# A hybrid decoder block in one core: who requests the down products' weights, and where the activations land

## The chip, the cores and the metric

The kernel runs on one NeuronCore of a Trainium2 chip. The metric is the device time of one execution in microseconds. All times are read from executions on the chip: three runs for the time, and one profiled execution for the trace.

The five engines run side by side and meet only at semaphores. TensorE (PE) multiplies, ScalarE (ACT) and VectorE (DVE) work on rows of tiles, GpSimd (POOL) and SyncE (SP) here mostly request transfers. A transfer is requested by an engine in its own program order: an engine that waits for a semaphore requests nothing that stands behind the wait.

## The reference

The reference is one decoder layer on 2048 tokens of width 1024, in float32: attention, a gated chunk mixer and a state-space layer, an output projection, then a gated feed-forward part with a causal convolution, a gated embedding and a last normalisation. The change touches only the feed-forward part:

```python
def conv_ffn(x, w_up, conv_w, conv_b, w_down):
    h = x @ w_up                      # 2048x1024 @ 1024x5632
    h = lax.conv_general_dilated(h, conv_w[:, None, :], ...) + conv_b
    val, gate = jnp.split(h, 2, axis=-1)
    return (jax.nn.gelu(gate) * val) @ w_down   # 2048x2816 @ 2816x1024
...
    h = h + conv_ffn(rms_norm(h, norm_ffn_g[i]), ffn_w_up[i], ffn_conv_w[i],
                     ffn_conv_b[i], ffn_w_down[i])
```

## The kernel before

Every float32 operand of a product is split in two float32r tiles, hi (a rounded copy, by ACT) and lo (the rest, by DVE), and each product is three matmuls: hi by hi, hi by lo, lo by hi.

`feed_forward` works in two halves of 1024 tokens. Each half has an up part and a down part.

The **up part** goes over 22 features (128 columns of value and 128 of gate each). A feature is seven products of twelve matmuls (kinds 1 to 7, a Strassen-like scheme over two token groups and two halves of the depth), in an order that `FIRST` gives for the first feature and `products` for the rest. Kinds 3, 4, 5, 6 and 7 take their activation operand from tiles of their own, `x3` to `x7` (a hi and a lo half each; the lo half holds the exact value until it is overwritten). Sums of weights are made in `sums`. The results go through the convolution in `strips` and are stored to DRAM (`ffn_act`) from `late` by POOL, two stores a feature.

The **down part** is four passes (two token groups by two halves of the 1024 output columns). A pass goes over the 22 features; each is twelve matmuls on four banks. The weights come in units of four features, 1 MB each, six units a pass (the last has two features, 0.5 MB). They land in `w`, two buffers that units take in turn; a unit is split by `split_unit` (one ACT and one DVE instruction) into one of two regions of `ring`, which is free once the last feature of the unit before last is multiplied. The activations of a feature, 256 KB, are loaded from `ffn_act` (`load_a`) and split by `split_a` into one of four slots (`a_hi`, `a_lo`; tiles `a_early` and `a_late`). The buffer that an activation lands in (`a_exact`) is the same memory as the slot's lo half: the split overwrites it in place, and PE reads it. So the load of activation a+4 waits until PE has finished feature a (`wait_feature_done`).

What sets the order of the work around the change is written out by hand, one program per engine:

- SP requests in one sequence the weights (`load_w_after`, which waits until the unit that held the buffer is split, `w_lo_ready`), the activations (`load_a`), the residual rows of each pass (`load_resid`, 1 MB, in the unit j = 2), in half 0 the input rows of the next half (`load_rows`, 2 MB each, at two places), and in half 1 ahead of pass 1 the eight 512 KB pieces of the weights of the last stage (`w_gate_loads`, 4 MB).
- ACT and DVE split activations `AHEAD` = 2 features ahead of the one whose turn it is, with the unit split (`split_unit` of the next unit) ahead of them at the start of each unit. At the end of the up part (`j == N - 1`) they split the first four (`RING`) activations before the last feature's convolution is done.
- PE waits for the unit's and the activation's lo half (`w_lo_ready`, `a_lo_ready`).
- POOL stores the activations of the half, then one 1 MB result per pass.

Half 0's down part also prepares half 1: the rows are squared, scaled, turned by PE (`turn`, eight times eight transposes in passes 1 and 3) and split; the last three operands, kinds 6, 7 and 4, in `split_sums`.

Of the kernel before, what the change touches and what calls it, by code (L numbers as in the profile page):

```python
# [22 lines left out]
P = 128  # L23
# [1637 lines left out]
def feed_forward(nc, h1, gain, w_up, conv_w, conv_b, w_down, h2, act_rows, w_gate_loads, shared, ident):  # L1661
# [45 lines left out]
    LO_NEEDED = {1: 2 * KH, 2: 2 * KH, 5: 4 * KH, 3: 4 * KH, 6: 4 * KH + 1, 7: 4 * KH + 2, 4: 4 * KH + 3}  # L1707
# [4 lines left out]
    with Stage(nc, "ffn") as st:  # L1712
        halves_of = shared.rearrange("p (o s k t) -> p o s k t", o=2, s=2, k=KH)
        own, exact = {}, {}
        for kind in (3, 4, 5, 6, 7):
            own[kind] = st.sb(f"x{kind}", [P, 2, KH, BANK], F32R)
            exact[kind] = st.over(f"exact{kind}", [P, KH, BANK], F32, nc.sbuf_base - KH * BANK * 4)
        x_hi = {1: halves_of[:, 0, 0], 2: halves_of[:, 1, 0], **{kind: t[:, 0] for kind, t in own.items()}}
# [21 lines left out]
        a_exact = [sums[:, 1], sums[:, 3], plain[:, BANK:2 * BANK], plain[:, 3 * BANK:4 * BANK]]  # L1740
# [7 lines left out]
        w_loaded = st.sems("w_loaded", 2)  # L1748
# [7 lines left out]
        a_loaded = st.sems("a_loaded", RING)  # L1756
# [17 lines left out]

        def loads_through(W):
            return sum((2 if v % UNITS < F else 1) for v in range(W % 2, W + 1, 2)) * DMA

        def wait_raw(engine, W):
            engine.wait_ge(w_loaded[W % 2], loads_through(W))
# [26 lines left out]
        def last_of_half(h):  # L1806
            return (h + 1) * PASSES * F
# [22 lines left out]

        @block.sync
        def _(sp):
# [4 lines left out]
            def load_w(W):  # L1837
                h, u = divmod(W, UNITS)
                if u < F:
                    for n in range(2):  # L1840
                        col = (n * F + u) * P
                        sp.dma_start(w_raw[W % 2][:, n], up_cols[:, :, col:col + P]).then_inc(w_loaded[W % 2], DMA)
                else:
                    p, j = divmod(u - F, PER_PASS)
                    fs, cols = unit_features[j], slice(p % NH * BANK, (p % NH + 1) * BANK)
                    flat = w_raw[W % 2].rearrange("p n k c -> p (n k c)")[:, 0:len(fs) * BANK]
                    sp.dma_start(flat.rearrange("p (f c) -> p f c", c=BANK), down_rows[:, fs[0]:fs[-1] + 1, cols]).then_inc(w_loaded[W % 2], DMA)

            def load_w_after(W):
# [893 lines left out]
```

## Time and profile before

| | us |
|---|---|
| median of 3 runs | 2889.83 (2889.22 to 2890.85) |
| the profiled execution | 2886.86 |
| its span, first to last instruction | 2885.3 |
| TensorE busy in the span | 2607.5 (90%) |
| VectorE, ScalarE, GpSimd busy | 1712.4, 1368.2, 509.6 |
| down part of half 0 | 1659.0 to 1923.2 |
| down part of half 1 | 2345.0 to 2605.0 |
| last stage | from 2605.0 |

The profiled execution is 3.0 us below the median of the runs, with 1.6 us around its span. Times within the span are counted from its first instruction. A row of the timeline gives the start, the duration, the engine, the line, what it writes and reads, and in brackets the idle time before it with what ended it. Matmuls are pipelined: their durations overlap, and the distance between two starts tells the rate.

### The profile page before, as it was taken

To read this page: it belongs to the slowest core of one execution; us is meant where nothing else is said; L and a number is where in the kernel's file an instruction comes from. 1 tells how busy PE (TensorE), PEld (TensorE's weight loads), DVE (VectorE), ACT (ScalarE), POOL (GpSimd) and SP (SyncE) were. 2 spreads that over 40 slices of the span, in tenths; PEclk is the share of its full clock that TensorE was granted. 3 is DMA by queue.
4 is the path that set the end of the run, shared out by engine and by line. 5 is a ranking of instruction groups with operands and counts; after the bars stand their busy time and mean duration, and the time that the engine had idled before them with its cause. 6 is when DMAs were issued, how large, how long until landed. Compare 5 with 4: busy or idle time off the path is not lost. (4 is left out here: it accounts for less than half of the span.)

```text
span 2885.3 us, 38789 instructions
## 1 busy us (share of the span) xinstructions
PE 2607.5 (90%) x13883; PEld 2239.3 (78%) x13883; DVE 1712.4 (59%) x3358; ACT 1368.2 (47%) x2460; POOL 509.6 (18%) x309
## 2 busy tenths in 40 slices
PE   6999997999845799489999999999999998997998
PEld 5989986999834588478888777778888876775876
DVE  1110272777596776488888755578888864444333
ACT  3343332666423666455555444455555542334444
POOL 3454454666300121000000000000000000000000
PEclk9999998999977799789999999999999999998999
DMA  4665456888333253312222366642222246662221
GB/s 163 195 213 172 152 170 157 188 185 185 70 100 126 87 182 129 104 59 88 88 81 75 116 208 232 224 146 88 88 81 75 87 152 245 223 205 99 79 76 46
DMA packets 313909, 392.09 MB, mean 136 GB/s; under 512 B 22161, under 2 KB 222161, under 8 KB 310650
## 3 DMA queue, kind: packets, MB, share of 16 engines
q1 hardware_dynamic: 299850, 341.60, 39.2%
q0 software_dynamic: 13888, 48.25, 4.3%
q8 instruction: 103, 1.69, 0.2%
q14 instruction: 68, 0.56, 0.1%
HBM read 298.59 MB, written 95.33 MB: 137 GB/s over the span
## 5 line engine op out<-in xcount | busy, mean ns | idle before, releaser
L2355 PE MATMUL ffn_bank<-ffn_x,ffn_ring 128*128 128x512 f32 x880 | 346.0, 393 | 19.1 <-DVE ffn_ring L2149 13.6
L2356 PE MATMUL ffn_bank<-ffn_x,ffn_ring 128*128 128x512 f32 x880 | 345.4, 393 | 0.0
L2357 PE MATMUL ffn_bank<-ffn_x,ffn_ring 128*128 128x512 f32 x880 | 345.4, 392 | 0.0
L504 ACT ACTIVATE att_exps<-att_scores,att_part 128x256 f32<-128x256 f32 (+1 forms) x384 | 153.1, 454 | 124.4 <-DVE att_part L475 121.7
L2355 PEld LDWEIGHTS ffn_bank<-ffn_x,ffn_ring 128*128 128x128 f32 x880 | 166.8, 190 | 55.8 <-DVE ffn_ring L2149 9.1
L475 DVE CUSTOM_DVE_ANT_0 att_scores<-att_bank,att_bias 128x256 f32<-128x256 f32 (+1 forms) x384 | 122.5, 363 | 141.3 <-PE att_bank L422 66.1
L2422 POOL DMA_DIRECT2D ffn_act<-ffn_late x88 | 47.6, 541 | 858.7 <-DVE ffn_late L2201 858.7
L2188 DVE SCALAR_TENSOR_TENSOR ffn_strips<-ffn_strips,ffn_taps 128x512 f32<-128x512 f32 x176 | 132.0, 750 | 111.9 <-ACT ffn_strips L1999 111.9
L938 POOL TENSOR_TENSOR in_w_lo<-in_w,in_w_hi 128x2048 fp32r<-128x2048 f32 x36 | 166.0, 4612 | 183.3 <-ACT in_w_hi L821 183.3
L2357 PEld LDWEIGHTS ffn_bank<-ffn_x,ffn_ring 128*128 128x128 f32 x880 | 166.8, 190 | 34.9
L2356 PEld LDWEIGHTS ffn_bank<-ffn_x,ffn_ring 128*128 128x128 f32 x880 | 166.9, 190 | 34.5
L908 PE MATMUL in_bank<-in_w_hi,in_hi 128*128 128x256 f32 x640 | 184.6, 288 | 0.7 <-issue 0.7
L909 PE MATMUL in_bank<-in_w_lo,in_hi 128*128 128x256 f32 x640 | 183.2, 286 | 0.0
L910 PE MATMUL in_bank<-in_w_hi,in_lo 128*128 128x256 f32 x640 | 183.2, 286 | 0.0
L1985 ACT COPY ffn_strips<-ffn_bank 128x512 f32<-128x512 f32 x176 | 103.3, 587 | 141.8 <-PE ffn_bank L2357 141.8
L449 PE MATMUL att_bank<-att_v,att_expsT 128*128 128x66 f32 x1200 | 153.1, 269 | 1.9 <-DVE att_expsT L486 1.3
L1956 ACT CAST ffn_ring<-ffn_sums 128x512 fp32r<-128x512 f32 x176 | 108.0, 614 | 94.5 <-PE ffn_bank L2357 83.8
L2387 PE MATMUL ffn_bank<-ffn_ring,ffn_a_late 128*128 128x512 f32 x352 | 139.8, 397 | 13.9 <-DVE ffn_a_late L2163 13.8
L2387 PE MATMUL ffn_bank<-ffn_ring,ffn_a_early 128*128 128x512 f32 x352 | 139.8, 397 | 11.2 <-DVE ffn_a_early L2163 11.1
L2157 DVE TENSOR_TENSOR ffn_ring<-ffn_w,ffn_ring 128x2048 fp32r<-128x2048 f32 (+1 forms) x48 | 101.5, 2114 | 81.0 <-ACT ffn_ring L1965 80.9
L449 PEld LDWEIGHTS att_bank<-att_v,att_expsT 128*128 128x128 f32 x1200 | 146.6, 192 | 3.7 <-DVE att_expsT L486 2.0
L2355 PE MATMUL ffn_bank<-tail_shared,ffn_ring 128*128 128x512 f32 x352 | 138.0, 392 | 1.0 <-DVE ffn_ring L2149 1.0
(337 smaller groups left out, 7004.0 us busy)
## 6 DMA issues: line engine op xcount, KB each, us to landing
ffn_w<-in_ffn_w_up SPq DMA_DIRECT2D x88, 512.0 KB, 4.7
ffn_w<-in_ffn_w_down SPq DMA_DIRECT2D x40, 1024.0 KB, 7.1
in_w<-in_w_in SPq DMA_DIRECT2D x36, 1024.0 KB, 6.2
ffn_act<-ffn_late POOLq DMA_DIRECT2D x88, 256.0 KB, 2.7
ffn_sums<-ffn_act SPq DMA_DIRECT2D x88, 256.0 KB, 4.5
ffn_strips<-ffn_act SPq DMA_DIRECT2D x88, 256.0 KB, 4.5
mixed_part<-branch_results SPq DMA_DIRECT2D x16, 792.0 KB, 5.3
z_rows<-in_result SPq DMA_DIRECT2D x80, 128.0 KB, 2.5
```

Of the source, the lines that this page charges most:

```text
L449: mm = pe.matmul(out, expsT[:, n % 2, piece * P:(piece + 1) * P], vals[:, b, blk, h * ROW:(h + 1) * ROW], start=(at == 0), stop=(at == len ...
L475: nc.vector.tensor_tensor_reduce(scores[:, n % RING, m * width:(m + 1) * width], score_bank[n % 3][:, m * width:(m + 1) * width], bias[pai ...
L504: nc.scalar.activation(exps[:, n % RING, m * width:(m + 1) * width], scores[:, n % RING, m * width:(m + 1) * width], ACT.Exp, bias=part[:, ...
L908: pe.matmul(out[:, 0:WIDE], x_hi[:, k, part], w_hi[w][:, k, :], start=(k == 0), stop=False)
L909: pe.matmul(out[:, 0:WIDE], x_hi[:, k, part], w_lo[w][:, k, :], start=False, stop=False)
L910: mm = pe.matmul(out[:, 0:WIDE], x_lo[:, k, part], w_hi[w][:, k, :], start=False, stop=(k == KC - 1))
L938: nc.gpsimd.tensor_tensor(w_lo[B % 2][:, :, :], w_raw[B % 2][:, :, :], w_hi[B % 2][:, :, :].bitcast(F32), ALU.subtract).then_inc(w_lo_read ...
L2188: nc.vector.scalar_tensor_tensor(conv[:, n, tg], raw[f % 2][:, n, 1 + tg * BANK:1 + (tg + 1) * BANK], tap[1], conv[:, n, tg], ALU.mult, AL ...
L2355: pe.matmul(out[:, :], hi[:, k], x_hi[kind][:, k], start=(k == 0 and fresh), stop=False, skip_group_check=not fresh)
L2356: pe.matmul(out[:, :], hi[:, k], x_lo[kind][:, k], start=False, stop=False, skip_group_check=not fresh)
L2357: mm = pe.matmul(out[:, :], lo[:, k], x_hi[kind][:, k], start=False, stop=(k == KH - 1), skip_group_check=not fresh)
L2387: pe.matmul(out, a_hi[r][:, toks], ring[:, first + i], start=(f == 0), stop=False)
```

## The change

The activations get landing buffers of their own, `a_raw`: four buffers of 256 KB in the memory of the hi half of `x6`, which no product reads from the last kind 6 product of the up part on. The split reads `a_raw` and writes the slot. A load now waits only until the activation four before it is split (`a_lo_ready`), and the wait for PE moves from the load to the split (ACT, in `split_a`). `AHEAD` becomes 3, and three instead of four activations are split at the end of the up part; the fourth comes in the down part, behind `split_unit` of unit 1.

The weights of the down units from the third on, and the first two up weights of half 1, are requested by POOL (`load_w_after(pool, ...)`), behind its last activation store of the half; the pass results are stored behind the second such request of the next pass. The loads have two semaphores per queue. SP keeps the activations, the residual rows and the input rows. The eight pieces of the last stage's weights are no longer requested in a row but one per unit (j other than 2) from the start of pass 1 of half 1.

Since `x6` is taken until the last activation of half 0 is split, its `split_sums` comes last of the three in half 1 (`LAST_SUMS`), two features later than before (`FINISH_AT`), and the first feature of half 1 runs its kinds in the order 1, 5, 2, 3, 6, 7 instead of 1, 5, 6, 3, 2, 7.

```diff
-    AHEAD = 2
+    AHEAD = 3
     RING = 4
+    RAW = 4
...
-    TURN_AT, FINISH_AT = (2, 6, 10, 14), (15, 17, 18, 19)
-    FIRST = ((1, 2, 5, 3, 6, 7), (1, 5, 6, 3, 2, 7))
+    TURN_AT, FINISH_AT = (2, 6, 10, 14), (15, 17, 18, 20)
+    FIRST = ((1, 2, 5, 3, 6, 7), (1, 5, 2, 3, 6, 7))
+    LAST_SUMS = ((6, 7, 4), (7, 4, 6))
...
+            if kind == 6:
+                a_raw = st.over("a_raw", [P, RAW, BANK], F32, nc.sbuf_base - 2 * KH * BANK * 4)
...
-        a_exact = [sums[:, 1], sums[:, 3], plain[:, BANK:2 * BANK], plain[:, 3 * BANK:4 * BANK]]
...
-        w_loaded = st.sems("w_loaded", 2)
+        w_loaded = [st.sems("w_loaded_sp", 2), st.sems("w_loaded_pool", 2)]
...
+        def by_pool(W):
+            return int(W >= 2 and (W - 2) % UNITS >= F)
...
+        def load_w_after(queue, W):
+            h, u = divmod(W, UNITS)
+            if W + 2 < HALVES * UNITS:
+                queue.wait_ge(w_lo_ready, operand_count(h, at[h][u, 4]) if u < F else unit_count(h, u - F))
+                load_w(queue, W + 2)
...
             def load_a(a):
                 h, p, f = feature(a)
                 o = (h * F + f) * TG + p // NH
-                r = a % RING
-                if a >= h * PASSES * F + RING:
-                    wait_feature_done(sp, *divmod(a - RING, F))
-                elif r < 2:
-                    sp.wait_ge(w_lo_ready, operand_count(h, at[h][F - 1, 7]))
+                if a >= h * PASSES * F + RAW:
+                    sp.wait_ge(a_lo_ready, a - RAW + 1)
                 else:
-                    sp.wait_ge(conv_ready, (h * F + F - 1) * 4)
+                    sp.wait_ge(product_done, h * N + at[h][F - 1, 6] + 1)
                 sp.wait_ge(act_stored[o % RING], (o // RING + 1) * DMA)
                 col = h * PART + p // NH * BANK
-                sp.dma_start(a_exact[r], act_rows[f][:, col:col + BANK]).then_inc(a_loaded[r], DMA)
+                sp.dma_start(a_raw[:, a % RAW], act_rows[f][:, col:col + BANK]).then_inc(a_loaded[a % RAW], DMA)
...
-                    if h + 1 == HALVES and p == 1:
-                        sp.wait_ge(product_done, HALVES * N)
-                        for part, src, loaded in w_gate_loads:
-                            sp.dma_start(part, src).then_inc(loaded, DMA)
                     for j, fs in enumerate(unit_features):
-                        load_w_after(h * UNITS + F + p * PER_PASS + j)
                         for f in fs:
-                            a = (h * PASSES + p) * F + f + RING
+                            a = (h * PASSES + p) * F + f + RAW
...
+                        if h + 1 == HALVES and p in (1, 2) and j != 2 and p * PER_PASS + j < 2 * PER_PASS + 4:
+                            n = (p - 1) * (PER_PASS - 1) + j - (j > 2)
+                            part, src, loaded = w_gate_loads[n]
+                            if n == 0:
+                                sp.wait_ge(product_done, HALVES * N)
+                            sp.dma_start(part, src).then_inc(loaded, DMA)
...
             def split_a(a):
-                r = a % RING
-                act.wait_ge(a_loaded[r], (a // RING + 1) * DMA)
-                nc.scalar.copy(a_hi[r], a_exact[r]).then_inc(a_hi_ready, 1)
+                h, p, f = feature(a)
+                act.wait_ge(a_loaded[a % RAW], (a // RAW + 1) * DMA)
+                if a >= h * PASSES * F + RING:
+                    wait_feature_done(act, *divmod(a - RING, F))
+                elif a % RING < 2:
+                    act.wait_ge(w_lo_ready, operand_count(h, at[h][F - 1, 7]))
+                else:
+                    act.wait_ge(conv_ready, (h * F + F - 1) * 4)
+                nc.scalar.copy(a_hi[a % RING], a_raw[:, a % RAW]).then_inc(a_hi_ready, 1)
...
                     if j == N - 1:
-                        for a in range(first, first + RING):
+                        for a in range(first, first + AHEAD):
                             split_a(a)
...
                 for p in range(PASSES):
-                    store(h * PASSES + p)
+                    for j in range(PER_PASS):
+                        load_w_after(pool, h * UNITS + F + p * PER_PASS + j)
+                        if p and j == 1:
+                            store(h * PASSES + p - 1)
+                store(h * PASSES + PASSES - 1)
```

Three places of the instruction order follow, of before and of the change apart.

SP in half 1, from the request of a unit in pass 0 to pass 1. `tail_w_gate` is the last stage's weights, `ffn_late` the residual rows; `ffn_sums` and `ffn_strips` are the old landing buffers of the activations. Before:

```order
L1847 DMA ffn_w<-in_ffn_w_down 128x4x512
L1867 DMA ffn_sums<-ffn_act 128x512 x2
L1899 DMA tail_w_gate<-in_ple_w_gate 128x1024 x8
L1847 DMA ffn_w<-in_ffn_w_down 128x4x512
L1867 DMA ffn_strips<-ffn_act 128x512 x2
```

And in the change, all of SP's requests from unit j = 2 of pass 0 to unit j = 3 of pass 1:

```order
L1880 DMA ffn_late<-after_mixers 128x4x512
L1870 DMA ffn_a_raw<-ffn_act 128x512 x14
L1914 DMA tail_w_gate<-in_ple_w_gate 128x1024
L1870 DMA ffn_a_raw<-ffn_act 128x512 x4
L1914 DMA tail_w_gate<-in_ple_w_gate 128x1024
L1870 DMA ffn_a_raw<-ffn_act 128x512 x4
L1880 DMA ffn_late<-after_mixers 128x4x512
L1870 DMA ffn_a_raw<-ffn_act 128x512 x4
L1914 DMA tail_w_gate<-in_ple_w_gate 128x1024
```

The requests of weights are gone from SP, and the eight pieces stand one by one between groups of activations.

POOL in the whole feed-forward part. Before it holds the load of the gain and the stores alone:

```order
L2431 DMA ffn_gain<-in_norm_ffn_g 128x8x1
L2422 DMA ffn_act<-ffn_late 128x512 x44
L2428 DMA after_ffn<-ffn_late 128x4x512 x4
L2422 DMA ffn_act<-ffn_late 128x512 x44
L2428 DMA after_ffn<-ffn_late 128x4x512 x4
```

In the change, from the up part of half 1 on, passes 0 and 1:

```order
L2434 DMA ffn_act<-ffn_late 128x512 x44
L1847 DMA ffn_w<-in_ffn_w_down 128x4x512 x3
L1847 DMA ffn_w<-in_ffn_w_down 128x2x512
L1847 DMA ffn_w<-in_ffn_w_down 128x4x512 x4
L2440 DMA after_ffn<-ffn_late 128x4x512
L1847 DMA ffn_w<-in_ffn_w_down 128x4x512
L1847 DMA ffn_w<-in_ffn_w_down 128x2x512
```

The first request of a weight unit stands behind the 44th store of the half.

ACT at the end of the up part and the start of the down part. `ffn_a_early` and `ffn_a_late` are the slots (two each), `ffn_ring<-ffn_w` with 2048 columns is a unit's split, the rows with `ffn_taps` and `ffn_strips` are the last feature's convolution and gelu. Before:

```order
L1965 CAST ffn_ring<-ffn_w 128x2048
L1971 CAST ffn_a_early<-ffn_sums 128x512 x2
L1971 CAST ffn_a_late<-ffn_strips 128x512 x2
L1999 ACTIVATE ffn_strips<-ffn_strips,ffn_taps 128x512 x2
L1985 COPY ffn_strips<-ffn_bank 128x512
L1999 ACTIVATE ffn_strips<-ffn_bank,ffn_taps 128x512
L1999 ACTIVATE ffn_strips<-ffn_strips,ffn_taps 128x512
L2004 ACTIVATE ffn_strips<-ffn_strips 128x512 x2
L1965 CAST ffn_ring<-ffn_w 128x2048
L1971 CAST ffn_a_early<-ffn_sums 128x512 x2
```

In the change:

```order
L1971 CAST ffn_ring<-ffn_w 128x2048
L1983 CAST ffn_a_early<-ffn_a_raw 128x512 x2
L1983 CAST ffn_a_late<-ffn_a_raw 128x512
L2011 ACTIVATE ffn_strips<-ffn_strips,ffn_taps 128x512 x2
L1997 COPY ffn_strips<-ffn_bank 128x512
L2011 ACTIVATE ffn_strips<-ffn_bank,ffn_taps 128x512
L2011 ACTIVATE ffn_strips<-ffn_strips,ffn_taps 128x512
L2016 ACTIVATE ffn_strips<-ffn_strips 128x512 x2
L1971 CAST ffn_ring<-ffn_w 128x2048
L1983 CAST ffn_a_late<-ffn_a_raw 128x512
L1983 CAST ffn_a_early<-ffn_a_raw 128x512 x2
```

The fourth activation has moved from ahead of the last convolution to behind the split of unit 1. DVE has the same order.

## Rows read from the trace of the kernel before

**Rows 1.** Windows of the down parts: PE, PEld, DVE, ACT, POOL, clock, DMA, GB/s.

```profile
1659.00:1923.20 264.20, 253.16 (x1121) 206.12 (x1119) 151.90 (x177) 126.33 (x168) 3.35 (x5) 0.99 0.64 213
...
2345.00:2605.00 260.00, 244.79 (x1057) 199.22 (x1055) 118.69 (x132) 93.04 (x112) 3.35 (x5) 0.97 0.62 210
```

**Rows 2.** The timeline of PE around the down parts.

```profile
1900.35 1.04 PE L2324 MATMUL ffn_bank<-whole_ident,ffn_strips 128*128 128x128 f32 x8
...
1923.29 0.51 PE L2355 MATMUL ffn_bank<-tail_shared,ffn_ring 128*128 128x512 f32 x1 [1.03 <-DVE ffn_ring L2149]
...
2344.99 0.39 PE L2387 MATMUL ffn_bank<-ffn_ring,ffn_a_early 128*128 128x512 f32 x1
...
2350.43 0.39 PE L2387 MATMUL ffn_bank<-ffn_ring,ffn_a_late 128*128 128x512 f32 x1
...
2428.08 0.77 PE L2387 MATMUL ffn_bank<-ffn_ring,ffn_a_late 128*128 128x512 f32 x1 [10.01 <-DVE ffn_a_late L2163]
```

**Rows 3.** Waits of PE: us in total, times, longest; half 0's down part.

```profile
PE ffn_bank L2387 <- DVE ffn_a_early L2163: 7.6, 5, 4.0
PE ffn_bank L2387 <- DVE ffn_a_late L2163: 2.2, 2, 1.9
```

**Rows 4.** The same view of waits, half 1's down part.

```profile
PE ffn_bank L2387 <- DVE ffn_a_late L2163: 11.6, 3, 10.0
PE ffn_bank L2387 <- DVE ffn_a_early L2163: 3.5, 5, 1.4
```

**Rows 5.** Windows around the two longest waits of PE.

```profile
2412.00:2430.00 18.00, 7.70 (x29) 6.01 (x30) 4.89 (x9) 3.40 (x4) 0.76 (x1) 0.73 1.01 396
2428.00:2434.00 6.00, 5.92 (x14) 4.72 (x15) 4.06 (x4) 2.68 (x3) 0.00 (x0) 0.52 0.32 123
1685.00:1700.00 15.00, 14.98 (x59) 12.27 (x60) 5.60 (x7) 7.07 (x9) 0.00 (x0) 0.89 0.37 125
```

**Rows 6.** Waits of ACT in half 1's down part.

```profile
ACT ffn_a_late L1971 <- DMA ffn_strips<-ffn_act: 78.6, 26, 15.4
```

**Rows 7.** The timeline of ACT and DVE at the start of half 0's down part.

```profile
1664.16 1.90 ACT L1965 CAST ffn_ring<-ffn_w 128x2048 fp32r<-128x2048 f32 x1
...
1666.09 2.29 DVE L2157 TENSOR_TENSOR ffn_ring<-ffn_w,ffn_ring 128x2048 fp32r<-128x2048 f32 x1 [1.04 <-ACT ffn_ring L1965]
1668.30 1.35 DVE L2163 TENSOR_TENSOR ffn_a_early<-ffn_sums,ffn_a_early 128x512 fp32r<-128x512 f32 x2
```

**Rows 8.** The timeline of SP's requests ahead of the two longest waits.

```profile
1670.50 1.93 SPq L1835 DMA_DIRECT2D ffn_strips<-after_mixers  x4
...
1673.72 2.17 SPq L1867 DMA_DIRECT2D ffn_sums<-ffn_act  x2
...
2405.99 4.37 SPq L1899 DMA_DIRECT2D tail_w_gate<-in_ple_w_gate  x8
```

**Rows 9.** DMA issues of the page: KB each, median us to landing.

```profile
ffn_w<-in_ffn_w_down SPq DMA_DIRECT2D x40, 1024.0 KB, 7.1
ffn_act<-ffn_late POOLq DMA_DIRECT2D x88, 256.0 KB, 2.7
after_ffn<-ffn_late POOLq DMA_DIRECT2D x8, 1024.0 KB, 6.2
```

**Rows 10.** All instances of two lines: min, median, max duration in ns.

```profile
L2428 POOL DMA_DIRECT2D after_ffn<-ffn_late x8: 752/756/762, 1734.7 to 2608.3; - x8
L2088 DVE TENSOR_SCALAR ffn_strips<-ffn_strips,ffn_rstd x14: 747/748/754, 1187.3 to 1849.8; 128x1024 f32<-128x1024 f32 x14
```

**Rows 11.** POOL's last store of half 0's up part.

```profile
1665.35 0.54 POOL L2422 DMA_DIRECT2D ffn_act<-ffn_late  x1 [0.32 <-DVE ffn_late L2201]
```

**Rows 12.** DVE at the start of half 1's down part.

```profile
2354.91 1.29 DVE L2163 TENSOR_TENSOR ffn_a_early<-ffn_sums,ffn_a_early 128x512 fp32r<-128x512 f32 x2
```

**Rows 13.** DVE just before the up part of half 1.

```profile
1917.69 2.29 DVE L2120 TENSOR_TENSOR ffn_x<-ffn_exact,ffn_x 128x2048 fp32r<-128x2048 f32 x1
```

**Rows 14.** PE in the first feature of half 0.

```profile
1249.43 0.47 PE L2355 MATMUL ffn_bank<-ffn_x,ffn_ring 128*128 128x512 f32 x1 [0.77 <-ACT ffn_strips L1985]
```

More of the change, by code:

```diff
@@ L1706, in feed_forward @@
     LO_HALF, SUM_HALF = 4 * KH + 3, 3 * KH + 1
-    LO_NEEDED = {1: 2 * KH, 2: 2 * KH, 5: 4 * KH, 3: 4 * KH, 6: 4 * KH + 1, 7: 4 * KH + 2, 4: 4 * KH + 3}
+    LO_NEEDED = [{1: 2 * KH, 2: 2 * KH, 5: 4 * KH, 3: 4 * KH, **{kind: 4 * KH + n + 1 for n, kind in enumerate(last)}} for last in LAST_SUMS]
     up_cols = w_up.rearrange("(k p) n -> p k n", p=P)
@@ L1773, in unit_count @@
             return h * (N + DOWN_UNITS) + N + u + 1
+        def by_pool(W):
+            return int(W >= 2 and (W - 2) % UNITS >= F)
         def loads_through(W):
-            return sum((2 if v % UNITS < F else 1) for v in range(W % 2, W + 1, 2)) * DMA
+            return sum((2 if v % UNITS < F else 1) for v in range(W % 2, W + 1, 2) if by_pool(v) == by_pool(W)) * DMA
         def wait_raw(engine, W):
-            engine.wait_ge(w_loaded[W % 2], loads_through(W))
+            engine.wait_ge(w_loaded[by_pool(W)][W % 2], loads_through(W))
         def wait_feature_done(engine, n, f):
@@ L1835, in load_rows @@
                     sp.dma_start(rows_of(h, grp, t), row_tiles[(h * TG + grp) * TILES + t]).then_inc(rows_loaded[grp][t], DMA)
[L1837 to L1849, printed above, removed]
-                h, u = divmod(W, UNITS)
-                if W + 2 < HALVES * UNITS:
-                    sp.wait_ge(w_lo_ready, operand_count(h, at[h][u, 4]) if u < F else unit_count(h, u - F))
-                    load_w(W + 2)
             def load_a(a):
@@ L1942, in split_sums @@
             def split_sums(h, n):
-                act.wait_ge(x_summed, h * SUM_HALF + 3 * KH + (1 if n == 2 else 0))
-                kind = (6, 7, 4)[n]
+                kind = LAST_SUMS[h][n]
+                act.wait_ge(x_summed, h * SUM_HALF + 3 * KH + (1 if kind == 4 else 0))
+                if h and kind == 6:
+                    act.wait_ge(a_lo_ready, last_of_half(h - 1))
                 nc.scalar.copy(x_hi[kind], exact[kind][:, :, :]).then_inc(hi_written, 1)
@@ L2032, in _ @@
                     if j == N - 1:
-                        for a in range(first, first + RING):
+                        for a in range(first, first + AHEAD):
                             split_a(a)
@@ L2117, in split_sums @@
             def split_sums(h, n):
-                kind = (6, 7, 4)[n]
+                kind = LAST_SUMS[h][n]
                 dve.wait_ge(hi_written, h * LO_HALF + 4 * KH + n + 1)
@@ L2248, in _ @@
                     if j == N - 1:
-                        for a in range(first, first + RING):
+                        for a in range(first, first + AHEAD):
                             split_a(a)
```

28 lines of the change are left out of this document (20 added, 8 removed).

## The prediction

> **What bounds the kernel now.** I read the windows first. The two down parts take 264.2 and 260.0 us with PE at a granted clock of 0.99 and 0.97 and the DMA engines busy 64% and 62% of the time [rows 1]. In the timeline, 24 down matmuls start from 2344.99 to 2350.43, so one takes 0.2267 us [rows 2]; 4 passes of 22 features of 12 matmuls are 1056, or 239.4 us. Half 0 has eight turns on top, 1.04 us each [rows 2], 8.3 us. What is left is loss: 264.2 - 239.4 - 8.3 = 16.5 us, and 260.0 - 239.4 = 20.6 us, together 37.1 us.
>
> Then the waits of PE. It waits for the activations' split only, never for a down unit: 7.6 + 2.2 = 9.8 us in half 0 [rows 3], 11.6 + 3.5 = 15.1 us in half 1 [rows 4], and 1.03 us for the first weight operand of half 1 [rows 2]: 25.9 us. Behind the two long waits the granted clock falls to the lower level (1.2 instead of 2.4 GHz): 0.52 over 6 us is 2.9 us lost, 0.89 over 15 us is 1.7 us [rows 5]. The last 6.6 us are small gaps and restarts.
>
> Then who is late. ACT in half 1 waits for activations to land, 78.6 us in 26 waits for one kind of slot [rows 6]: DVE and ACT are not the bound, the transfers are. The reason is the loop: activation a+4 is requested when PE has finished a, and has three features, 3 x 2.72 = 8.2 us, to land and be split; with ACT's and DVE's share 1.3 us (DVE's two splits in 1.35 us [rows 7], so 0.7 each) some 6.8 us for landing. The longest waits stand behind bursts: the eight pieces of 4 MB requested at 2405.99 to 2410.36, with the DMA engines at 1.01 and 396 GB/s, end in PE's 10.01 us; 2 MB of rows at 1670.50, one row of the queue ahead of the activations at 1673.72, end in the 4.0 us of half 0 [rows 2, 3, 5, 8].
>
> **The change, part by part.** *Landing buffers and three ahead.* The request of a+4 now follows the split of a, which ACT may do when PE has finished a-4. So it goes out some 7 features less a split ahead of its use, 19 - 1.4 = 17.7 us, instead of 8.2. The split itself can start three features (8.2 us) ahead of its use. At a unit's start ACT splits the unit (1.90), DVE too (2.29), then the activation (0.7) [rows 7]: 4.9 us, inside 8.2; before it was inside 5.4, which is where the waits under 2 us come from. I cost these waits at nothing left, except for remainders below.
>
> *Weights by POOL.* A unit is requested when the one in its buffer is split, some 4.9 us after the start of the unit before; ACT wants it at the second unit start from there, 2 x 10.9 - 4.9 = 16.9 us later. A load by POOL doesn't occur in this stretch; the nearest rows are its stores of the same 1 MB and pieces, 0.756 us to issue and 6.2 us to land, against 7.1 for SP's load of a unit [rows 9, 10]. I take 6 to 7 us; under 16.9 it costs nothing. At the start of a down part POOL comes to its first request behind the last store, at 1665.35 + 0.54 = 1665.9 [rows 11]. Landed by 1673, split by 1678; PE wants it at feature 8, 1659.0 + 21.8 = 1680.8. Hidden, by 3 us. But 1 MB now moves into the time of the 2 MB of rows: with unit 3 and the activations 4.5 MB from 1665.9, 11.4 us at 396 GB/s [rows 5], until 1677.3. Activation 8 lands there, and PE wants it at 1680.8 plus the delay below. I cost it at nothing, at most 4.
>
> *Eight pieces apart.* A unit of 10.9 us then carries 1 MB of weights, 1 MB of activations and 0.5 MB: 240 GB/s of the 396 seen. The 10.01 us and the 2.9 us of clock go.
>
> *Three instead of four splits at the start.* This one costs. The fourth activation stands behind unit 1's split on DVE, where the fifth stood: ready at 1668.30 + 0.68 = 1669.0 [rows 7]. PE wants it at 1659.0 + 8.2 = 1667.2: a wait of 1.8 us. In half 1: 2354.91 + 0.7 = 2355.6 against 2345.0 + 8.2 = 2353.2, 2.4, less 0.6 for the split that no longer stands ahead of DVE's unbroken chain: 1.8 [rows 12]. Together 3.7 with the semaphores.
>
> *Half 1's start.* DVE's third 2.29 us split stood at 1917.69, just ahead of the sums of the first weights [rows 13]; it moves behind the first operands, so the 1.03 us wait goes. Kinds 6 and 7 now follow each other on one bank, as in half 0, where PE waited 0.77 us for ACT's copy of the bank between them [rows 14]: +0.9 with the restart.
>
> *Sum.* 37.1 lost now; left are 3.7 + 0.9, and I keep 2.5 of the small gaps and of clock behind the two new waits (bounds: 0, and the 6.6 + 4.6 that stand there now). 37.1 - 7.1 = 30.0 gained. The profiled execution of 2886.9 becomes 2856.9; the median of the runs stands 3.0 above it: 2859.8, say 2860. Own range 2852 to 2871.
>
> On the second queue, the trace shows the engines full at 396 GB/s when SP alone requests [rows 5]. The Trainium skill (DMA: Bandwidth & Descriptors, "Issuing engines are not separate DMA queues") says that transfers of all issuing engines run on the same 16 DMA engines and that another issuer saves only issue time. By that rule the queue split gives no bandwidth; the sum would stand, since it rests on earlier requests, or fall to rival 1 if they give nothing.
>
> **Rivals.** 1: *the transfers stay as late as they are.* Waits come from full engines, and asking earlier only queues more: the small waits stay, only the burst of 4 MB is spread. That saves 10.0 + 2.9 and costs 3.7 + 0.9: 8.3 gained, 2881 or 2882; with half the small waits gone 2875. For it: 64% mean load with bursts, and a burst at half 0's start that is now 1 MB fuller. Against it: between the bursts 213 GB/s is half of what the engines did, and the loop's 8.2 us explains the small waits without any shortage.
>
> 2: *POOL's loads land late* (the slower side). If a unit takes L from request to landing, two units need L + 4.9 us per buffer, and PE needs on average 19.9 us for two (a pass is 59.8 us for six units). From L = 15 on each us costs 22 us over the 22 pairs. At L = 17 that is 44 - 30: 2904; at 20, 2970; at 16.4 the gain is eaten. For it: no load of this shape by POOL is in the trace, and DVE works all through. Against it: POOL's 88 stores took a median of 2.7 us with DVE at its busiest, and the 1 MB stores 6.2 [rows 9]; L would have to be more than double. The Trainium skill (SBUF — State Buffer, "SBUF: two separate sides") speaks for it: a DMA requested by GpSimd has its descriptors written by GpSimd, which a VectorE operation in a two-port mode locks out until it ends. What could do so here are the row scalings, four in a row of 0.75 us twice in half 0 [rows 10]: 3.0 us late on a unit that has 10 to spare, so by the rule the sum stands; it would need the same from the 2.29 us splits to bring this rival in, and for these the page says there is no two-port mode.
>
> 3: *the gain is given back at the starts.* The first units and activation 8 come late in both halves by up to 4 us each, the clock falls behind each wait (1.7 each), and some small waits stay: 2884 to 2890. For it: margins of 3 us at the start. Against it: in half 1 no rows are loaded there.
>
> **How the numbers follow.** Forecast 0.70; rival 1 0.14 (2873 to 2882); rival 3 0.07; rival 2 0.09. A difference under 0.2% (5.8 us) can't be told from none. Faster: forecast, rival 1 and a fifth part of the others, with a little off for what I haven't seen, 0.84; same 0.07; slower 0.09. The range that leaves out 2 in 10 is 2850 to 2882: below it would lie only a sum in which no loss at all remains and the up parts gain too.
>
> **What would show it.** Right: in PE's waits the down parts hold one wait of about 1.8 us each at feature 3 and next to nothing else; the parts take about 250 and 243 us; the 10 us wait is gone and the granted clock is 0.99 or more in both; POOL's loads of a unit land in 6 to 8 us; a wait of 0.8 us between kinds 6 and 7 in half 1. Wrong: PE waits for `ffn_ring` of a unit in the down parts (rival 2), or ACT still waits some 50 us for landings with PE's small waits in place (rival 1), or a wait of several us at features 7 to 9 of half 0 (rival 3).

## The result and the profile after

The changed kernel takes 2856.12 us in the median of five runs (2854.08 to 2860.05), against 2889.83 before: 0.9886 of the time, with a 95% interval of 0.9871 to 0.9900. Run again later on another occasion, it took 2856.95 against 2889.53 (0.9891, 0.9875 to 0.9908). The profiled execution took 2856.12 us, 30.7 less than the profiled one of before; the forecast for it was 30.0 less. Among all executions behind this document a single one, of the kernel e6 below, took 6817 us; it is left out of the numbers.

The windows of the down parts in the changed kernel; behind the length stand the busy times of PE, weight loads, DVE, ACT and POOL, then the granted clock, the DMA share and GB/s. They answer to [rows 1, 5]; the third is the start of half 0's down part.

```profile
1658.00:1911.10 253.10, 249.02 (x1121) 205.71 (x1120) 150.49 (x178) 126.96 (x167) 23.32 (x31) 0.99 0.67 224
2333.70:2575.10 241.40, 239.66 (x1057) 197.96 (x1055) 117.98 (x132) 93.77 (x113) 19.76 (x27) 1.00 0.67 228
1665.00:1684.00 19.00, 15.24 (x66) 11.96 (x65) 8.11 (x8) 5.15 (x8) 2.13 (x3) 1.00 0.96 356
```

The parts take 253.1 and 241.4 us where they took 264.2 and 260.0: 29.7 of the 30.7 us. Over what the matmuls and turns need (247.7 and 239.4), 5.4 and 2.0 us are left of 37.1. Outside the down parts, the first down product starts 1.0 us earlier (1658.0 against 1659.0), the up part of half 1 is 0.9 us longer (422.6 against 421.7), and the last stage, from the end of the down part to the end of the span, is 0.9 us shorter (279.3 against 280.2).

All waits of PE from the last product of the first up part to the end of the second down part, in its timeline:

```profile
1653.59 0.47 PE L2367 MATMUL ffn_bank<-ffn_x,ffn_ring 128*128 128x512 f32 x1 [2.36 <-DVE ffn_strips L2185]
...
1668.01 0.50 PE L2399 MATMUL ffn_bank<-ffn_ring,ffn_a_late 128*128 128x512 f32 x1 [1.66 <-DVE ffn_a_late L2175]
...
1684.33 0.47 PE L2399 MATMUL ffn_bank<-ffn_ring,ffn_a_early 128*128 128x512 f32 x1 [2.42 <-DVE ffn_a_early L2175]
...
1925.63 0.47 PE L2367 MATMUL ffn_bank<-ffn_x,ffn_ring 128*128 128x512 f32 x1 [0.77 <-ACT ffn_strips L1997]
...
2330.82 0.47 PE L2367 MATMUL ffn_bank<-ffn_x,ffn_ring 128*128 128x512 f32 x1 [2.36 <-DVE ffn_strips L2185]
...
2343.72 0.50 PE L2399 MATMUL ffn_bank<-ffn_ring,ffn_a_late 128*128 128x512 f32 x1 [1.74 <-DVE ffn_a_late L2175]
```

Of sixteen waits in and between the down parts [rows 2 to 4] four are left: the fourth activation at each start (1668.01, 2343.72), activation 8 (1684.33), and kind 7 behind kind 6 (1925.63). The two of 2.36 us close the up parts; they were there before.

Who is waited for on ACT, half 1's down part (total us, times, longest), against [rows 6]:

```profile
ACT ffn_ring L1971 <- PE ffn_bank L2401: 43.6, 21, 2.1
ACT ffn_a_late L1983 <- PE ffn_bank L2401: 32.5, 21, 2.1
ACT ffn_a_early L1983 <- PE ffn_bank L2401: 26.3, 18, 2.1
ACT ffn_a_early L1983 <- DMA ffn_a_raw<-ffn_act: 16.6, 8, 3.3
ACT ffn_a_late L1983 <- DMA ffn_a_raw<-ffn_act: 12.4, 8, 3.4
```

Beside the 78.6 us of [rows 6], ACT had this wait for the other kind of slot before:

```profile
ACT ffn_a_early L1971 <- DMA ffn_sums<-ffn_act: 52.5, 24, 4.4
```

This is the view that tells what bounds the part: ACT waited 131.1 us for activations to land and now waits 29.0 us for them, but 102.4 us for PE.

The DMA issues (KB each, median us to landing), against [rows 9]:

```profile
ffn_a_raw<-ffn_act SPq DMA_DIRECT2D x176, 256.0 KB, 6.3
...
ffn_w<-in_ffn_w_down POOLq DMA_DIRECT2D x36, 1024.0 KB, 9.3
```

Both kinds of loads take longer from request to landing than before (an activation took 4.5 us, a unit 7.1), and it costs nothing where they are requested early enough.

### The profile page after: what moved, and what is told of

It is laid out like the page before. It is cut to its first block and busy times, and to the rows that moved or that the text cites. A ratio compares the mean times of both kernels' runs of the same rounds, so it can differ in the third digit from the quotient of the medians.

```text
span 2854.5 us, 38966 instructions
## 1 busy us (share of the span) xinstructions
PE 2597.1 (91%) x13883; PEld 2235.7 (78%) x13883; DVE 1710.4 (60%) x3358; ACT 1369.3 (48%) x2460; POOL 545.8 (19%) x357
## 5 line engine op out<-in xcount | busy, mean ns | idle before, releaser
L2399 PE MATMUL ffn_bank<-ffn_ring,ffn_a_early 128*128 128x512 f32 x352 | 138.5, 393 | 2.4 <-DVE ffn_a_early L2175 2.4
L2401 PE MATMUL ffn_bank<-ffn_ring,ffn_a_early 128*128 128x512 f32 x352 | 137.7, 391 | 0.0
## 6 DMA issues: line engine op xcount, KB each, us to landing
in_w<-in_w_in SPq DMA_DIRECT2D x36, 1024.0 KB, 6.2
ffn_w<-in_ffn_w_down POOLq DMA_DIRECT2D x36, 1024.0 KB, 9.3
```

Source lines behind the costliest of these rows:

```text
L2399: pe.matmul(out, a_hi[r][:, toks], ring[:, first + i], start=(f == 0), stop=False)
L2401: mm = pe.matmul(out, a_lo[r][:, toks], ring[:, first + i], start=False, stop=(f == F - 1))
```

## The experiments

Each was timed in alternation with the kernel before (medians 2891.1 for the first four, 2886.7 for the next four, 2889.5 for the last three). Runs of one kernel in one group differ by up to 9 us (2885.88 to 2895.05 for before in the first group). A part of this lies ahead of all that the edits touch: the first up product started between 1210.5 and 1215.9 us in the profiled executions. So an edit worth 2 or 3 us is read from the length of the down parts in one profiled execution each. They repeat more closely: the change gave 253.1 and 241.4 us once, 253.4 and 241.4 again, and before and e2, whose programs are the same in half 0, gave 264.3 and 265.5 there.

| kernel | median us | ratio to before (95%) | down part 0 | down part 1 |
|---|---|---|---|---|
| before | 2889.83 | | 264.3 | 260.0 |
| change | 2856.12 | 0.9886 (0.9871 to 0.9900) | 253.1 | 241.4 |
| e1 weights by SP | 2860.93 | 0.9894 (0.9879 to 0.9909) | 251.1 | 241.4 |
| e2 before, pieces apart | 2880.57 | 0.9958 (0.9944 to 0.9972) | 265.5 | 251.4 |
| e3 pieces in a row | 2858.28 | 0.9886 (0.9871 to 0.9901) | 253.6 | 243.9 |
| e4 four at the start | 2857.00 | 0.9878 (0.9863 to 0.9893) | 254.5 | 239.4 |
| e5 rows two and two | 2853.90 | 0.9888 (0.9872 to 0.9904) | 248.8 | 241.4 |
| e6 three edits | 2852.52 | 0.9882 (0.9863 to 0.9901) | 249.6 | 239.4 |
| e7 two ahead | 2861.62 | 0.9916 (0.9902 to 0.9930) | 253.5 | 246.9 |
| e8 before, three ahead | 2898.36 | 1.0039 (1.0025 to 1.0053) | 279.9 | 254.0 |
| change again | 2856.95 | 0.9891 (0.9875 to 0.9908) | 253.4 | 241.4 |
| e9 e6 with e1 | 2850.85 | 0.9870 (0.9853 to 0.9886) | 248.4 | 239.6 |
| e10 e9, unit behind add | 2849.08 | 0.9865 (0.9848 to 0.9881) | 250.7 | 241.6 |

The parts are measured from the first down matmul to the next part's first matmul (half 0), or to the end of the last one.

**e1: is the second queue worth anything?**

```diff
         def by_pool(W):
-            return int(W >= 2 and (W - 2) % UNITS >= F)
+            return 0
...
                     for j, fs in enumerate(unit_features):
+                        load_w_after(sp, h * UNITS + F + p * PER_PASS + j)
                         for f in fs:
...
                     for j in range(PER_PASS):
-                        load_w_after(pool, h * UNITS + F + p * PER_PASS + j)
```

> The change with the down units' weights back in SP's sequence, one request at the start of each unit as before; landing buffers, three ahead and the pieces apart stay. My theory (the gain comes from requesting an activation seven features ahead instead of three, and from the pieces apart; the second queue adds nothing by itself): SP reaches the request of a unit at about the time POOL does, some 4.9 us into the unit before, so the time stays within 3 us of the change, 2853 to 2859, with no waits of PE beyond the start waits; the wait of 2.4 us at feature 8 of half 0 gets shorter, since unit 2 is then requested before the rows. Rival (the separate queue is what does it): activations behind 1 MB units in one queue come late again, PE has its waits under 2 us back, 2866 or more.

Down part 1 is the same to the tenth, down part 0 is 2.0 us shorter. The median is 1.9 us over the upper end of what I expected; the profiled execution was already 4.1 us behind the change's at the first up product (1215.9 against 1211.8), where the two programs are the same, and this part is no effect of the queue. PE's waits in down part 0 (total us, times, longest):

```profile
PE ffn_bank L2400 <- DVE ffn_a_late L2176: 1.7, 1, 1.7
PE ffn_bank L2337 <- DVE ffn_late L2221: 0.8, 1, 0.8
PE ffn_bank L2337 <- issue: 0.6, 1, 0.6
PE ffn_bank L2400 <- DVE ffn_a_early L2176: 0.5, 1, 0.5
```

The wait for activation 8 fell from 2.42 to 0.5 us, and no small waits for activations came back; two waits of the turns (L2337), 0.8 and 0.6 us, are new. And its DMA issues:

```profile
ffn_a_raw<-ffn_act SPq DMA_DIRECT2D x176, 256.0 KB, 5.9
ffn_w<-in_ffn_w_down SPq DMA_DIRECT2D x40, 1024.0 KB, 6.9
```

With one queue a unit lands in 6.9 us, with POOL's in 9.3, and activations are not late behind units. The move of the weights to POOL's queue, by which the change is named, is not what gained the time; in the down parts the second queue brought no speed. What it may be worth lies in the last stage, about a microsecond: that stage took 279.0 to 279.3 us in the seven profiled kernels in which POOL requests the weights and 279.9 to 280.4 in the six in which SP does. Why was not looked into.

**e2: what are the pieces apart worth by themselves?** The kernel before, with the eight pieces requested as in the change:

```diff
-                    if h + 1 == HALVES and p == 1:
-                        sp.wait_ge(product_done, HALVES * N)
-                        for part, src, loaded in w_gate_loads:
-                            sp.dma_start(part, src).then_inc(loaded, DMA)
...
+                        if h + 1 == HALVES and p in (1, 2) and j != 2 and p * PER_PASS + j < 2 * PER_PASS + 4:
+                            ...
+                            sp.dma_start(part, src).then_inc(loaded, DMA)
```

> The kernel before, with only the eight 512 KB pieces requested one per unit from pass 1 of half 1 instead of in a row. My theory: the 10.0 us wait, its restart and the 2.9 us of low clock behind it go, the small waits stay and one or two grow: 12 to 14 us gained, 2876 to 2878. Rival (the buffers would have absorbed the burst anyway, or the pieces only move the wait): less than 6 us gained, or waits of 2 us at each of the eight pieces, 2884 or more. If nearly all of the gain came from here: 2862 or less.

The median fell by 10.6 us, under the 12 to 14 expected, and down part 1 by 8.6. The 10.01 us wait is gone, but 12.0 us of loss are left in the part. Its timeline of PE holds:

```profile
2431.60 0.47 PE L2389 MATMUL ffn_bank<-ffn_ring,ffn_a_late 128*128 128x512 f32 x1 [1.20 <-DVE ffn_a_late L2165]
...
2478.17 0.80 PE L2389 MATMUL ffn_bank<-ffn_ring,ffn_a_late 128*128 128x512 f32 x1 [2.63 <-DVE ffn_a_late L2165]
```

The first stands at a down feature where before had no wait, the second at one where before waited 1.15 us. Behind the second the granted clock fell:

```profile
2478.20:2488.20 10.00, 10.00 (x32) 7.99 (x32) 4.25 (x7) 2.57 (x3) 0.76 (x1) 0.69 0.57 195
```

That is 3.1 us more. It explains most of why the part gained 8.6 us and not the 10.0 + 2.9 of the long wait. That the pieces made these two activations late is likely but not shown: in half 0, where the two programs are the same, one wait went from 0.88 to 3.79 us between the two executions.

**e3: does the lead absorb the burst?** The change, with the eight requests in a row ahead of pass 1 of half 1 as before (the edit of e2 reversed).

> The change with the eight pieces requested in a row again, ahead of pass 1 of half 1. My theory: an activation is requested 17.7 us ahead, the burst of 4 MB takes about 11 us at 396 GB/s, with a unit and the activations in it 14 us; so PE waits 0 to 4 us in place of 10.0: 2856 to 2861. Rival (the burst costs what it cost before, whatever the lead): the wait of 10 us and its low clock are back, 2868 to 2870.

```profile
2411.79 0.47 PE L2397 MATMUL ffn_bank<-ffn_ring,ffn_a_late 128*128 128x512 f32 x1 [2.02 <-DVE ffn_a_late L2173]
```

It does: where the burst cost a wait of 10.01 us and 2.9 us of clock, it costs a wait of 2.02 us, and down part 1 is 2.5 us longer than the change's. The median can't tell it from the change (0.9886 of before for both). So the pieces apart are worth 8.6 us without the lead and 2.5 with it; the two edits overlap.

**e7: what does the third feature ahead do?** The change with `AHEAD = 2`.

> The change with activations split two features ahead instead of three (two at the end of the up part); landing buffers, POOL's requests and the pieces apart stay. My theory (the landing buffers carry most: a request goes out six features ahead instead of three, and the split needs 4.9 us of 5.4 behind a unit's split): PE gets waits under 1 us at some of the 44 unit starts, and the start wait is larger, since the third activation stands behind unit 1's split too: 4.4 us in each half, 2.7 more than now. Down parts 256 to 258 and 244 to 247: 2862 to 2869. Rival (three ahead is what does it, the buffers little): waits at most unit starts, 2876 or more.

Its timeline of PE in the down parts holds three waits, two of which are the starts:

```profile
1667.38 0.80 PE L2399 MATMUL ffn_bank<-ffn_ring,ffn_a_late 128*128 128x512 f32 x1 [4.38 <-DVE ffn_a_late L2175]
...
1899.82 0.50 PE L2399 MATMUL ffn_bank<-ffn_ring,ffn_a_early 128*128 128x512 f32 x1 [0.35 <-DVE ffn_a_early L2175]
...
2343.42 0.80 PE L2399 MATMUL ffn_bank<-ffn_ring,ffn_a_late 128*128 128x512 f32 x1 [4.40 <-DVE ffn_a_late L2175]
```

The start waits are the 4.4 us expected, and of the small waits one of 0.35 us is left. The ratio to before is 0.9916, where the change has 0.9886 and 0.9891. Down part 1 is 5.5 us longer than the change's: 2.7 us are the longer start wait, and the rest is the clock in the ten microseconds behind it, which in the change stays at 1.00:

```profile
2343.40:2353.40 10.00, 9.98 (x31) 7.98 (x32) 1.77 (x3) 1.32 (x1) 0.42 (x1) 0.69 0.88 290
```

From the fifth feature on each takes 2.72 us, as in the change. Down part 0 and the median (2861.62) came out a little under what I expected. So the buffers, with the requests as in the change, remove the small waits; the third feature ahead is worth the start wait and the clock behind it, and nothing in the steady part. In half 0 even that is hidden: what the start wait costs, the wait for activation 8, which is gone here, gives back (253.5 against 253.1 us).

**e8: three ahead without the buffers.** The kernel before with `AHEAD = 3`, in-place landing kept.

> The kernel before with the splits three features ahead instead of two, four at the start as before; activations still land in the slot's lo half, so their request waits for PE; pieces in a row. My theory (the loop request, landing, split is what was short, and splitting earlier cannot help what has not landed): within 5 us of before, 2885 to 2895, the 10 us wait in place. Rival (the order of ACT's and DVE's work was the bound, the small waits came from the activation standing behind a unit's split): the small waits go, 5 to 12 us gained, 2878 to 2885.

Both expectations fell: it is slower than before, by 0.39%. Down part 1 is 6.0 us shorter, and its small waits, 5.1 us in seven, are down to 0.65 in two, though the requests go out no earlier: the rival was right there, ACT's and DVE's order was part of the small waits. The long wait behind the burst stayed, with 8.78 us. But down part 0 grew by 15.6 us. Its waits of PE there:

```profile
PE ffn_bank L2387 <- DVE ffn_a_early L2163: 9.5, 3, 5.2
PE ffn_bank L2324 <- issue: 4.9, 1, 4.9
PE ffn_bank L2355 <- DVE ffn_ring L2149: 4.6, 1, 4.6
PE ffn_bank L2324 <- DVE ffn_late L2208: 2.9, 1, 2.9
```

L2324 is the turns: they wait for DVE's addition of the pass's result (L2208), and in DVE's order this now stands behind the split of an activation that has not landed. ACT's and DVE's timelines ahead of the 4.9 us wait:

```profile
1872.82 1.26 ACT L1971 CAST ffn_a_late<-ffn_strips 128x512 fp32r<-128x512 f32 x2 [2.64 <-DMA ffn_strips<-ffn_act]
```

```profile
1873.47 0.69 DVE L2163 TENSOR_TENSOR ffn_a_late<-ffn_strips,ffn_a_late 128x512 fp32r<-128x512 f32 x1 [2.02 <-ACT ffn_a_late L1971]
1874.08 2.48 DVE L2208 TENSOR_TENSOR ffn_late<-ffn_bank,ffn_late 128x512 f32<-128x512 f32 x4
```

The same goes for the first operand of half 1 (4.6 us). An engine in program order that waits for a landing delays all that stands behind it. In the change, with the buffers, three ahead costs nothing of this kind.

**e4: the start waits.**

```diff
-                        for a in range(first, first + AHEAD):
+                        for a in range(first, first + RING):
                             split_a(a)
...
-                            if a < last_of_half(h):
+                            if first + RING <= a < last_of_half(h):
                                 split_a(a)
```

> The change with four activations split at the end of the up part, as before, instead of three; the fifth is then the first behind unit 1's split. My theory (the start wait is the fourth activation behind the unit's split): both waits of 1.7 us at feature 3 go, 3 to 4 us gained against the change: 2852 to 2853. Rival (PE would wait for something else there, or the last convolution pays for the fourth split): same time as the change, with another wait within a microsecond of the old one.

Half 1 confirms it: no wait at all, 239.4 us, what the matmuls need. In half 0 the part did not get shorter (254.5 against 253.1 us), and the median, 2857.00, is over the 2852 to 2853 expected: the waits of 1.66 and 2.42 us became one of 4.60. In this kernel ACT waited 9.88 us for unit 2, with activation 7 behind it in its order; e6 and e9 come back to this.

```profile
1684.77 0.80 PE L2399 MATMUL ffn_bank<-ffn_ring,ffn_a_late 128*128 128x512 f32 x1 [4.60 <-DVE ffn_a_late L2175]
```

**e5: the transfers at the start of half 0.**

```diff
-                        if h + 1 < HALVES and p == 0 and j == 0:
-                            sp.wait_ge(act_ready, (h + 1) * F * TG)
-                            load_rows(h + 1, 0)
+                        if h + 1 < HALVES and p == 0 and j < 2:
+                            if j == 0:
+                                sp.wait_ge(act_ready, (h + 1) * F * TG)
+                            for t in (2 * j, 2 * j + 1):
+                                sp.dma_start(rows_of(h + 1, 0, t), row_tiles[(h + 1) * TG * TILES + t]).then_inc(rows_loaded[0][t], DMA)
```

> The change with the four 512 KB row loads of half 1's first group (2 MB) requested two and two, a unit apart, instead of in a row at the start of half 0's down part. My theory (the 2.4 us wait at feature 8 of half 0 comes from these 2 MB and the 2 MB of units 2 and 3 in one stretch, with the DMA engines 96% busy): the wait goes or falls under 0.7 us, down part 0 takes 250.5 to 251.5 instead of 253.1 us; total 2853 to 2855 where the change has 2856. Rival (activation 8 is late for its own request, which follows the split of activation 4): the wait stays at 2 us or more, down part 0 stays at 253.

The wait for activation 8 is gone and down part 0 is 248.8 us, 4.3 shorter, where the wait was 2.42. The rest is the clock: in the change it fell behind the wait, in this kernel it did not. The ten microseconds behind the wait, first in the change, then here:

```profile
1684.00:1694.00 10.00, 9.67 (x36) 7.83 (x37) 5.69 (x7) 5.85 (x8) 0.70 (x1) 0.83 0.49 136
```

```profile
1684.00:1694.00 10.00, 10.00 (x46) 8.26 (x44) 4.90 (x5) 4.46 (x8) 0.71 (x1) 1.00 0.85 302
```

A granted clock of 0.83 over ten microseconds is 1.7 us more, so this wait cost 4.1 to 4.3 us and not 2.4.

**e6: all three.** e4, e5 and `FIRST = (..., (1, 5, 2, 6, 3, 7))`.

> The change with three edits: four activations split at the end of the up part, the row loads two and two, and half 1's first feature in the order 1, 5, 2, 6, 3, 7, so that a product stands between kinds 6 and 7. My theory: down part 1 is 239.4 us, with no wait, as with the four splits alone; the 4.6 us wait of half 0, which the four splits alone left, goes with the burst of rows: down part 0 248 to 249; the 0.77 us wait in half 1's first feature goes. Together 6 to 7 us under the change: 2849 to 2851, and under 2.1 times 5.4 us of it from half 0. Rival (half 0's start is bound by the transfers in total, so every wait taken away comes back a feature later): down part 0 stays at 252 or more, 2853 to 2854.

The 0.77 us wait is gone and down part 1 is 239.4. Down part 0 is 249.6, 0.6 us over what I expected, and the median 2852.52 where I expected 2849 to 2851. One wait of 2.46 us is left there, and ACT's and POOL's timelines tell why:

```profile
1664.48 0.77 POOL L1847 DMA_DIRECT2D ffn_w<-in_ffn_w_down  x1
```

```profile
1674.44 1.91 ACT L1973 CAST ffn_ring<-ffn_w 128x2048 fp32r<-128x2048 f32 x1 [7.74 <-DMA ffn_w<-in_ffn_w_down]
1676.26 0.61 ACT L1985 CAST ffn_a_late<-ffn_a_raw 128x512 fp32r<-128x512 f32 x1
```

Unit 2 is requested behind POOL's last store, at 1664.5, and lands ten microseconds later; ACT waits 7.74 us for it, and activation 7, which has landed, stands behind it.

**e9: with that request early.** e6 with the edit of e1.

> The three edits of e6 (four splits at the start, rows two and two, a product between kinds 6 and 7) with all units requested by SP as in e1. What is tried: in e6 ACT waited 7.7 us for unit 2, which POOL requests only behind its last store, 10 us before it lands, and PE waited 2.5 us for activation 7 behind it. My theory: SP requests unit 2 some 10 us earlier, so this wait goes, and down part 0 is 247 to 248.5, down part 1 239.4 us: 6 to 9 us under the change on the same chip, 1 to 3 under e6. Rival (POOL's queue was worth something once the starts are mended): down part 0 at 250 or more, or waits of PE under 2 us scattered over both parts; not under e6.

SP requests unit 2 at 1653.2 us here, 11 us earlier than POOL did. No wait for activations is left in either part; 248.4 and 239.6 us, 0.7 and 0.2 over what the work needs. The median is 6.1 us under the change's in the same group of runs, 2850.85 against 2856.95, and its slowest execution (2852.40) is under the change's fastest (2856.40); their intervals against before overlap in part.

**e10: DVE's split of unit 0 behind the last addition.** e9, with `if j == N - 3:` made `if j == N - 2:` in DVE's program.

> e9 with DVE's split of unit 0 one place later, behind the addition that the last product of the up part waits for (PE waits 2.36 us there in every kernel so far). My theory: the addition is done 2.3 us earlier and the wait of 2.36 us goes in both halves, but the unit's split is then ready at the earliest 2.3 + 0.7 us behind product 7, and the activations behind it, where PE needs them 2.7 us behind: a wait of 0.5 to 1.5 us at feature 0 takes its place, 2 to 4 us gained on e9. Rival (the work only moves by a product, and the first activation's split behind the unit costs what was gained): the same time as e9 within 1 us, with 2 us or more of wait at feature 0.

The wait at the end of the up part fell from 2.36 to 0.88 us, and the up parts got 2.5 and 2.9 us shorter: the product behind the wait ran at a granted clock of 0.61 and 0.65 in e9, and runs at 1.00 here. What took its place is not at feature 0 but at feature 4, the fifth activation behind unit 1's split:

```profile
1666.89 0.47 PE L2402 MATMUL ffn_bank<-ffn_ring,ffn_a_early 128*128 128x512 f32 x1 [1.87 <-DVE ffn_a_early L2178]
```

PE comes 2.5 to 2.9 us earlier to an activation that is split no earlier. Most of the gain is given back, as the rival had it: 2849.08 us is the lowest median of all, but not told apart from e9.

## Why the prediction was right

**The sum held.** Predicted were 37.1 us of loss of which 7.1 stay; the trace gives 30.7 us gained in all and 29.7 in the down parts. The forecast of 2860 for the median is 3.9 us off, of which 3.0 is that I set the profiled execution of before under its median, while after the two are the same.

That the profiled difference came within 0.7 us is in part luck. What the sum covers, the down parts and half 1's first feature, gained 29.7 less the 0.9 us by which the up part of half 1 grew: 28.8. The rest came from the 1.0 us ahead of the first down product, where executions with the same program differ by more (it starts at 1658.0 us in the change and at 1660.7 in e3), and from 0.9 us in the last stage, which the prediction did not have. And the two parts were off in opposite directions: about 250 and 243 us were forecast, 253.1 and 241.4 came.

Two slips of the working change nothing: 19 less 1.4 is 17.6 us and not 17.7, and 4.5 MB in the sense of the profile's KB (1024.0 for a unit) take 11.9 us at 396 GB/s and not 11.4.

**The start waits** were priced at 1.8 each and are 1.66 and 1.74; e7 (4.4 each) and e4 (none at feature 3) show that their cause is the place behind unit 1's split.

**The wait between kinds 6 and 7** came as in half 0, 0.77 us; e6 removed it with a product in between. The 0.9 us by which half 1's up part grew fit the 0.9 of the sum, but executions in which this part has the same program differ by more (421.7 us in before and 423.1 in e2, 422.6 in the change and 424.1 in e5), so this size is not measured. **The 1.03 us wait** at half 1's first operand went.

**The small waits** went as predicted, but the reason given was half of it. The prediction took the loop of request, landing and split as too short. e8 shows that without any earlier request three ahead removes most of them in half 1 as well, since the activation no longer stands behind a unit's split at the last moment; e7 shows that the buffers, without the third feature ahead, remove them too. Either kind of slack suffices there. Only the kernels with the buffers do it in both halves. No run has the buffers without the other parts of the change; e1 and e3 take the queue and the pieces away one at a time and leave the small waits gone.

**The burst** of 4 MB: the two remedies in the change overlap (e2, e3). The prediction gave the whole 10.0 + 2.9 us to the pieces apart; alone they save 8.6 in that part, since another wait with its own 3.1 us of clock was there in e2.

**Mis-sized: the start of half 0.** "I cost it at nothing, at most 4" became 2.42 us of wait and 1.7 us of clock. The estimate moved 4.5 MB at 396 GB/s; the stretch from 1665 to 1684 ran at 356 GB/s with the engines 96% busy, which is 6.8 MB in 19 us, and ACT waited 9.3 us for activation 8. One load that the estimate left out is unit 4, which POOL requests inside the stretch:

```profile
1675.65 0.75 POOL L1847 DMA_DIRECT2D ffn_w<-in_ffn_w_down  x1 [7.24 <-DVE ffn_ring L2169]
```

e5 requests half of the rows later and e1 requests unit 2 before the rows, and each took the wait away or down to 0.5. So the sign that the prediction gave for rival 3, a wait at features 7 to 9 of half 0, did come, at this one place; the 2.5 us that the sum kept for gaps and clock took up most of it.

**Mis-sized: POOL's loads.** A unit takes 9.3 us from request to landing, not 6 to 7. It cost nothing in the steady part, where 15 would have begun to cost by the prediction's estimate, and it did cost in e6. So rival 2 (POOL's loads late) had a true premise that stayed under its threshold. The nearest rows were POOL's stores of 1 MB with 6.2 us. That they were stores does not explain the difference: in the changed kernel the same stores take as long as the loads. And POOL's loads of the last, half-size unit of a pass are no later than SP's were (7.9 us in before, 8.0 in e1):

```profile
after_ffn<-ffn_late POOLq DMA_DIRECT2D x8, 1024.0 KB, 9.4
...
ffn_w<-in_ffn_w_down POOLq DMA_DIRECT2D x8, 512.0 KB, 7.0
```

What the Trainium skill says of it (SBUF — State Buffer, "SBUF: two separate sides"), that a VectorE operation in a two-port mode keeps GpSimd from writing the descriptors of its DMAs, is shown by no run here in either direction: POOL's loads of 1 MB do land later, but what delays them was not separated.

**The rule on queues held.** That the transfers of all issuing engines run on the same 16 DMA engines and another issuer saves only issue time (the Trainium skill, DMA: Bandwidth & Descriptors, "Issuing engines are not separate DMA queues") agrees with e1: with one queue nothing was lost in the down parts (251.1 and 241.4 us against 253.1 and 241.4). Its consequence for this change is that the gain there came from what else is in it.

What stays open is why a unit of 1 MB lands later through POOL; e1 changes the queue and the times of the requests together.

## What to carry to other kernels

Let a load land in a buffer that is free when its reader's copy is made, not when the consumer of the copy is done: from e2 to e7, which differ in the landing buffers, the issuing queue (worth nothing there by e1), half 1's first order and the number of activations split at the end of the up part (two instead of four, which costs e7 its start waits), the down parts are 16.5 us shorter, with no faster transfer, and the sign that they were missing was an engine waiting for landings while the DMA engines were 64% busy. Where an in-order engine does both, ask what stands behind each wait for a landing, and move the first requests of a stage ahead of the last stores of the stage before. When several edits come together, undo each alone: the one that named this change did nothing in the parts it was meant for, and two others paid for the same wait.

## What the runs showed of the hardware

A 1 MB load took 6.9 us in the median from SP's queue (e1) and 9.3 us from POOL's (the change), with the same loads requested around it but at other times. POOL's stores of 1 MB took 6.2 us in before, 7.9 in e1 and 9.4 in the change, which differ in what else is requested, and by whom. A load of 512 KB of the same weights took 7.9 and 8.0 us from SP's queue (before, e1) and 7.0 from POOL's (the change). The DMA engines moved 356 GB/s at 96% busy at the start of half 0, against 396 at full load in the burst of before.

The granted clock of the ten microseconds behind a wait of PE was 0.69 or 0.70 after waits of 2.63, 4.40 and 4.60 us (e2, e7, e4), 0.83 after one of 2.42 (the change), but 1.00 after one of 2.46 us (e6) and after 1.74 and 2.02 us (the change, e3). So a wait can cost about twice its length, and its length alone does not tell whether it does.
